# Gated linear attention on one Trainium2 core: in the masked levels the vector engine merges a half's keys and queries ahead of its masked copies

## What is computed

```python
def gla_chunk_scan(q, k, v, log_g, state0, with_output):
    ...
    def step(state, inp):
        qc, kc, vc, gc = inp
        b = jnp.cumsum(gc.astype(jnp.float32), axis=2)
        b_last = b[:, :, -1:, :]
        new_state = (jnp.exp(b_last[:, :, 0, :])[..., None] * state
                     + jnp.einsum('bhsk,bhsv->bhkv', kc * jnp.exp(b_last - b), vc))
        ...
        diff = jnp.where(lower_tri, b[:, :, :, None, :] - b[:, :, None, :, :], -jnp.inf)
        a = jnp.einsum('bhtk,bhsk,bhtsk->bhts', qc, kc, jnp.exp(diff))
        o = (jnp.einsum('bhts,bhsv->bhtv', a, vc)
             + jnp.einsum('bhtk,bhkv->bhtv', qc * jnp.exp(b), state))
        return new_state, o
```

## Time and profile before

| | |
|---|---|
| Time, median of 3 runs | 2453.03 us (2452.18 to 2455.61) |
| The profiled execution's own time | 2453.45 us |
| Its span | 2451.7 us |
| PE busy | 2392.8 us, 98% |
| DVE busy | 1798.2 us, 73% |
| ACT busy | 1479.4 us, 60% |
| Masked copies, L1602 | 30, median 736 ns |
| Masked levels of layer 0, DVE | 222.35 to 242.3 us |
| Masked levels of layer 1, DVE | 815.62 to 827.7 us |

### The profile page before, as it was taken

How to read it: one execution, slowest core, us unless ns; L and a number is a source line. 1 busy time by engine, 2 the same in 40 slices (tenths; PEclk the granted TensorE clock), 3 DMA queues, 4 the chain that set the end, 5 groups by cost and what they waited for, 6 DMA issues and landing times.

```text
span 2451.7 us, 38334 instructions
## 1 busy us (share of the span) xinstructions
PE 2392.8 (98%) x14972; PEld 2037.2 (83%) x14972; DVE 1798.2 (73%) x2437; ACT 1479.4 (60%) x1950; POOL 27.8 (1%) x87
## 2 busy tenths in 40 slices
PE   8999999999999899999999999999999999999998
PEld 6876888888897688898888889898888888888886
DVE  5556666566566667677676658579898898998997
ACT  4245366465444566556675545667777777777776
POOL 0000000000000000010000001000000000000000
PEclk9999999999999999999999999999999999999999
DMA  8237245555544545554245545147998998999997
GB/s 333 105 146 272 108 164 188 187 184 189 188 161 150 224 175 187 188 194 159 87 150 194 189 172 199 70 155 292 372 358 340 371 358 339 370 362 348 360 361 271
DMA packets 81786, 565.11 MB, mean 230 GB/s; under 512 B 9345, under 2 KB 12689, under 8 KB 13777
## 3 DMA queue, kind: packets, MB, share of 16 engines
q1 hardware_dynamic: 80144, 559.97, 61.3%
q0 software_dynamic: 1472, 2.77, 0.4%
HBM read 560.49 MB, written 1.05 MB: 229 GB/s over the span
## 4 chain that ended last, share of the span: by engine, by line
PE 89%; DVE 4%; ACT 4%; issue 1%; DMA 1%; SPq 0%; ACTq 0%; DVEq 0%
PE psum L271 87%; ACT ring_hi L238 1%; DVE ring_lo L241 1%; PE psum L791 1%; PE psum L2642 1%; DMA Z<-in_first_mods 1%; ACT hT L844 1%; DVE hT L890 1%; DMA ring<-in_stream 0%; ACT turned_probs L854 0%; ACT Z L854 0%; DVE Z L1526 0%; DVE mixT L698 0%; DVE Z L1529 0%; DVE hT L468 0%
## 5 line engine op out<-in xcount | busy, mean ns | idle before, releaser
L241 DVE TENSOR_TENSOR ring_lo<-ring,ring_hi 128x2048 fp32r<-128x2048 f32 x474 | 1085.1, 2290 | 262.8 <-ACT ring_hi L238 257.5
L238 ACT ACTIVATE ring_hi<-ring 128x2048 fp32r<-128x2048 f32 x476 | 910.4, 1914 | 332.0 <-PE psum L271 326.4
L271 PE MATMUL psum<-h_parts,ring_hi 128*128 128x512 f32 (+1 forms) x3216 | 867.3, 349 | 5.5 <-DVE h_parts L478 2.6
L271 PE MATMUL psum<-h_parts,ring_lo 128*128 128x256 f32 (+1 forms) x2480 | 606.5, 291 | 0.0
L271 PEld LDWEIGHTS psum<-h_parts,ring_hi 128*128 128x128 f32 x3216 | 521.2, 190 | 31.9 <-issue 11.1
L271 PEld LDWEIGHTS psum<-h_parts,ring_lo 128*128 128x128 f32 x2480 | 469.9, 189 | 72.4
L271 PE MATMUL psum<-ring_hi,h_parts 128*128 128x512 f32 (+1 forms) x1856 | 523.4, 368 | 1.0 <-DVE h_parts L2631 0.6
L271 PEld LDWEIGHTS psum<-ring_hi,h_parts 128*128 128x128 f32 x1856 | 329.6, 189 | 54.6 <-ACT tok L348 0.8
L271 PE MATMUL psum<-ring_lo,h_parts 128*128 128x512 f32 (+1 forms) x928 | 338.5, 365 | 0.0
L271 PE MATMUL psum<-ring_hi,Zr 128*128 128x512 f32 (+1 forms) x736 | 225.3, 388 | 0.0
L271 PEld LDWEIGHTS psum<-ring_lo,h_parts 128*128 128x128 f32 x928 | 175.0, 189 | 28.7
(11 more groups left out here) (315 smaller groups left out, 2072.1 us busy)
## 6 DMA issues: line engine op xcount, KB each, us to landing
ring<-in_stream SPq DMA_DIRECT2D x524, 1024.0 KB, 4.8
Z<-in_first_mods SPq DMA_DIRECT2D x5, 1024.0 KB, 16.8
cst<-in_constants SPq DMA_DIRECT2D x1, 1216.0 KB, 8.0
mixT<-mixT POOLq DMA_DIRECT2D x32, 35.5 KB, 3.9
xT<-in_xT SPq DMA_DIRECT2D x1, 1024.0 KB, 5.8
xT<-in_ctxT SPq DMA_DIRECT2D x1, 1024.0 KB, 8.1
xT<-in_memT POOLq DMA_DIRECT2D x1, 1024.0 KB, 9.0
out_y<-hT SPq DMA_DIRECT2D x4, 256.0 KB, 2.8
```

The costliest lines, as they stand in the source:

```text
L238: e.activation(hi, raw, ACT.Copy).then_inc(sem("piece_rounded"), 1)
L241: e.tensor_tensor(lo, raw, hi.bitcast(F32), ALU.subtract).then_inc(sem("piece_split"), 1)
L271: ins = pe.matmul(*args, **kw)
```

## The change

In levels 0 to 3 the merge of a half now stands ahead of the half's copies, where it stood behind them. It waits for the grams of the half's last tile. In the last level that order was there already, and levels 4 and 5 have no copies. No instruction is added or taken away.

```diff
             for l in range(LEVELS):
                 mask = lvl_mask[:, min(l, MASKED - 1), :].unsqueeze(1).unsqueeze(1).to_broadcast([P, 2, 2, P])
                 for part, tiles in enumerate(halves_of(nt)):
+                    dve.wait_ge(sem("grams"), gr + nt * (l + 1) + tiles[-1] + 1)
+                    dve_merge(dve, layer, l, part).then_inc(sem("level" if l < LEVELS - 1 else "keys_decayed"), 1)
                     if l == LEVELS - 1:
-                        dve.wait_ge(sem("grams"), gr + nt * (l + 1) + tiles[-1] + 1)
-                        dve_merge(dve, layer, l, part).then_inc(sem("keys_decayed"), 1)
                         tiles = LAST_COPIES[layer][part]
                     for t in tiles:
                         dve.wait_ge(sem("grams"), gr + nt * (l + 1) + t + 1)
                         if MASKED - 1 <= l < LEVELS - 1:
                             continue
                         dve.wait_ge(sem("gram_read"), own + (nt * l + t + 1 if l < MASKED else nt * MASKED))
                         dve.copy_predicated(by_bank(t), mask, grams(t)).then_inc(sem("gram_read"), 1)
-                    if l < LEVELS - 1:
-                        dve_merge(dve, layer, l, part).then_inc(sem("level"), 1)
```

## The result

| | Time, median | Profiled execution's span |
|---|---|---|
| Before | 2452.98 us (7 runs, 2450.47 to 2455.61) | 2451.7 us |
| Changed | 2461.97 us (7 runs, 2459.34 to 2465.86) | 2462.4 us |

What follows compares the result with a forecast made beforehand. PE, holding 89% of the chain that ended last, was taken as the bound. Layer 0's levels at 6.79 against 5.15 us, plus 0.31 us once, and layer 1 at 0 gave +6.9 us: 2459.9 us, range 2457.0 to 2462.5.

Steps and rivals of the forecast that it cites:

- The walk through a level: Layer 0's masked levels: seven serial steps of PE grams, DVE merges, copies and handoffs, 6.79 us a level against 5.15.
- the two named: Layer 0's levels: PE waits for tile 0's copy before tile 3, and for the last copy before the next level's grams.
- The other sum on record: Layer 0's levels by the skill's DRAIN rule, without overlapping copies: about 7.3 us a level, change about +9.
- Layer 1 at nothing: Layer 1's levels: 1.4 us of delay goes into PE's wait for a transferred piece; 0, bounds 0 and +0.8 us.
- free swap: Rival, the levels: DVE bounds the stage, so order within a half doesn't matter; +0 to +1.6 us, chance 0.10.
- early keys: Rival, both layers' levels: ACT's gathering runs under the copies, its waits vanish; at most 1.5 us faster, chance 0.04.
- What I can't read: Behind level 4: PE's 1.81 us without a releaser, 0 or -1.8 us; later clock shifts, about 1 us either way.
- the unexplained stretch: PE behind layer 0's level 4, 1.81 us without a releaser: stays or goes, 0 or -1.8 us; going had chance 0.10.
- The clock in the levels: Rival, layer 0's levels 1 to 3: PE's gaps drop its clock to 1.2 GHz; +6.4 us, 2466, chance 0.08.
- the three pieces' 2.2 us: Layer 0's levels: at 1.2 GHz three weight pieces outgrow their cover, 2.2 us, said to apply in two levels.
- my signs of being wrong: Layer 0's levels 5.2 us apart, granted clock below 1.00 ahead of level 4, or lost time regained behind the levels.
- My argument against it: Layer 0's levels: PE kept clock 1.00 when busy 3.45 of 5 us at 805 to 810; here 62 to 75% busy.

Runs made afterwards that it cites:

- one half at a time: Kernel before, layer 0 only: merge ahead of its copies for just the first half (ratio 1.0022) or just the second half (1.001).
- tile 0's copy first: Kernel before, layer 0 only: first half's merge placed behind tile 0's copy and ahead of tile 1's, second half unchanged; ratio 1.0003.
- layer 1 alone: Kernel before with the merge moved ahead of the copies in layer 1 only; ratio 0.9998 (0.9989 to 1.0007).
- the repeat: The changed kernel measured once more, unaltered, on another chip; ratio to the kernel before 1.0029 (1.0019 to 1.0039).
- held slots: Ring slots of layer 0's level 3 weight pieces returned late: changed kernel 1.0035, kernel before 1.0004; levels 2 and 3 held, kernel before: 0.999 and 0.9996.
- its twin: Kernel before, slots of layer 0's five weight pieces of levels 2 and 3 given back with level 5's first matmuls; ratio 0.9996 (0.9987 to 1.0004).

## Why the prediction was right, and what it lacked

- **The walk through a level** (steps 1 to 7, 6.79 us) was right. Worked out: level 4 later by 6.88 us. Measured with the clock up: 6.88 and 6.87 us. That it fits to 0.01 us is luck: level 0 took 7.39 us where 7.10 was worked out, and levels 2 and 3 took 6.63 and 6.67 where 6.79 was, so errors of 0.3 us cancel. The waits are where they were said to be: DVE 1.34 us ahead of the first merge (forecast 1.4), PE 1.5 us ahead of tile 3, none for ACT. DVE's wait for tile 3 is 0.20 to 0.23 us in levels 1 to 3, where 0.4 was forecast. That each wait is one of the two named, and that the shared banks make the first, the runs with one half at a time and with tile 0's copy first show. The other sum on record, about +9 us with 7.3 us a level, lies as near to the measured time and is wrong in its cause: with the clock up, levels 1 to 3 took 6.63 to 6.78 us.
- **Layer 1 at nothing** was right, by cause as well: the wait for DMA shrank from 1.27 to 0.35 us, and the run with layer 1 alone gave 0.9998.
- **The free swap and the early keys** are ruled out. ACT's keys did come early, and gained nothing.
- **What lacked** was not in the levels' steps. The mis-sized term is the one under "What I can't read": the unexplained stretch was put at 0 or -1.8 us against before, and came out at +1.1 us in the profiled execution, -0.2 us in the repeat. I had listed no way for it to grow. The runs with held slots show that ring transfers queued ahead of a fetch of instructions make it. How the change moves the two against each other, and so what it adds to the stretch, stays open.
- **The clock in the levels** had a chance of 0.08 as a fall through all of them for +6.4 us. It fell for 3 us in level 0 of two profiles and not at all in two others with the same levels; the price was 0.6 to 0.7 us. The +6.4 us also counted the three pieces' 2.2 us once, where levels 1 and 3 both have three pieces, so that by its own terms it would have been +8.6. A granted clock below 1.00 ahead of level 4 was one of my signs of being wrong, and the first profile has it; it cost a tenth of what that rival charged, and the waits were those of the walk. My argument against it compared PE's busy share with one stretch that had kept the clock, and that comparison didn't decide it.
- **The two measurements** of the changed kernel, +9.1 us (6.9 to 11.3) and +7.1 us (4.7 to 9.6), both hold the 6.9 us, the first only at its lower end. What of their rest is the stretch and what is the clock changes from one execution to the next, and stays open.

## What to carry to other kernels

These runs bear out three habits. Ask of each instruction in an in-order queue who waits for it, and issue first what another engine is stopped on; a result wanted a little later is then free, as the merge behind the first copy was. Work that looks like a delay, a merge standing behind the copies, may be the cover under which the other engine makes the next input; moving it ahead leaves the same work and no cover. Where buffers are shared between tiles, look at the copy that frees a buffer first: here it was worth 4.8 us.

## What the hardware showed that was not expected

- PE ran dry at a boundary of 256 instructions in a place with very short matmuls (64 rows in 0.76 us), for 1.6 to 2.9 us, in the middle of a tile's matmuls, between which the kernel has no wait. The 16 KB packet started 2.2 to 2.5 us ahead of the stretch's end in ten profiles, and with transfers queued ahead of it 3.6 to 5.1 us after level 4's first row (nine of them). With the ring's transfers out of the way it started 1.1 to 1.2 us after that row and the stretch was gone (three kernels). What asks for it no row shows.
- Holding 5 MB of prefetch back, which made ACT wait 6.2 us, made the kernel faster by a hair, 0.999 (0.998 to 0.9999); its twin, with 4.25 us of waiting, came out at 0.9996 (0.9987 to 1.0004).
- The granted clock fell to 0.50 in level 0 in one execution of the changed kernel and stayed at 1.00 in another, with the same instructions. Behind the levels it was down for 7 to 10 us in the profiles with the stretch, and for about 3 us in those in which the held slots had removed it.
